# Feed-forward turns by 32-wide block transposes on VectorE and SBUF-to-SBUF transfers issued by GpSimd

## What is computed

```
def squared_relu_mlp(h, w1, w2):
    return jnp.square(jax.nn.relu(h @ w1)) @ w2      # w1: 2048 x 8192, w2: 8192 x 2048

x = x + squared_relu_mlp(rms_norm(x, norm_ffn_g[l]), w_ff1[l], w_ff2[l])
```

## Time and profile before

| what | value |
|---|---|
| runs of the kernel before | 1646.04 us median of 3 (1643.89 to 1647.24) |
| the profiled execution | 1646.18 us |
| its span | 1644.4 us |
| TensorE, matmuls busy | 1627.2 us, 99% of the span |
| VectorE busy | 1088.3 us, 66% |
| ScalarE busy | 811.9 us, 49% |
| GpSimd busy | 98.0 us, 6% (its DMA issues are not counted) |
| DMA | 304.91 MB, 185 GB/s over the span, of it 299.41 MB on SyncE's queue and 3.46 MB on GpSimd's |
| feed-forward stage | from about 945 us to about 1630 us |

### The profile page before, as it was taken

One profiled execution on the slowest core, in us unless ns is written; L12 is line 12 of the kernel. 1 busy time (PEld: TensorE's weight loads), 2 busy tenths in 40 slices (PEclk: granted clock), 3 DMA queues, 4 the chain that ended last, 5 costly groups with the idle time before them and its releaser, 6 DMA issues.

```text
span 1644.4 us, 21894 instructions
## 1 busy us (share of the span) xinstructions
PE 1627.2 (99%) x7524; PEld 1358.0 (83%) x7524; DVE 1088.3 (66%) x1476; ACT 811.9 (49%) x1063; POOL 98.0 (6%) x187
## 2 busy tenths in 40 slices
PE   9999999999999999999998999999999999999998
PEld 7888888888888888888887888888888888888886
DVE  5688988888888898665555655555555455545554
ACT  6444456555555556743445644434443444334443
POOL 6500011211111000000000000000000000000000
PEclk9999999999999999999999999999999999999999
DMA  7666655555555666557563566566656665566554
GB/s 249 207 185 187 190 160 159 174 169 181 172 155 172 221 201 182 189 180 268 177 194 115 168 182 190 191 194 190 186 188 191 191 182 188 193 192 184 192 184 142
DMA packets 158953, 304.91 MB, mean 185 GB/s; under 512 B 11658, under 2 KB 15874, under 8 KB 158466
## 3 DMA queue, kind: packets, MB, share of 16 engines
q1 hardware_dynamic: 157504, 299.41, 59.2%
q0 software_dynamic: 1056, 3.46, 0.6%
q10 hardware_dynamic: 320, 1.06, 0.2%
HBM read 301.78 MB, written 2.10 MB: 185 GB/s over the span
## 4 chain that ended last, share of the span: by engine, by line
PE 97%; ACT 1%; DVE 1%; issue 0%; POOL 0%; POOLq 0%; ACTq 0%
PE ps L1267 30%; PE ps L1269 30%; PE ps L1268 30%; PE ps L1280 2%; PE ps L1451 1%; PE ps L1450 1%; ACT hconv L750 0%; PE ps L1467 0%; PE ps L1461 0%; PE ps L1304 0%; PE ps L1555 0%; PE ps L1584 0%; PE ps L1583 0%; PE ps L1582 0%; PE ps L1468 0%
## 5 line engine op out<-in xcount | busy, mean ns | idle before, releaser
L868 DVE TENSOR_TENSOR wlo<-raw,whi 128x1024 fp32r<-128x1024 f32 x560 | 685.7, 1228 | 410.1 <-ACT whi L535 404.7
L535 ACT ACTIVATE whi<-raw 128x1024 fp32r<-128x1024 f32 x560 | 591.1, 1060 | 569.7 <-PE ps L1269 561.8
L1267 PE MATMUL ps<-whi,a_hi 128*128 128x512 f32 x1244 | 490.7, 394 | 0.6 <-issue 0.6
L1269 PE MATMUL ps<-whi,a_lo 128*128 128x512 f32 x1244 | 484.7, 390 | 0.0
L1268 PE MATMUL ps<-wlo,a_hi 128*128 128x512 f32 x1244 | 484.3, 389 | 0.0
L1267 PE MATMUL ps<-whi,c_hi 128*128 128x512 f32 x752 | 293.8, 391 | 0.0
L1269 PE MATMUL ps<-whi,c_lo 128*128 128x512 f32 x752 | 292.7, 389 | 0.0
L1268 PE MATMUL ps<-wlo,c_hi 128*128 128x512 f32 x752 | 292.6, 389 | 0.0
L1269 PEld LDWEIGHTS ps<-whi,a_lo 128*128 128x128 f32 x1244 | 233.5, 188 | 49.1
L1267 PEld LDWEIGHTS ps<-whi,a_hi 128*128 128x128 f32 x1244 | 233.7, 188 | 47.8 <-DVE wlo L868 1.2
L1268 PEld LDWEIGHTS ps<-wlo,a_hi 128*128 128x128 f32 x1244 | 233.8, 188 | 46.7
(11 more groups left out here) (240 smaller groups left out, 1081.8 us busy)
## 6 DMA issues: line engine op xcount, KB each, us to landing
raw<-in_w_ff_dram SPq DMA_DIRECT2D x256, 512.0 KB, 4.1
raw<-in_w_in_dram SPq DMA_DIRECT2D x144, 512.0 KB, 3.7
raw<-in_w_mla_out_dram SPq DMA_DIRECT2D x32, 512.0 KB, 4.6
raw<-in_w_conv_out_dram SPq DMA_DIRECT2D x32, 512.0 KB, 4.1
raw<-in_w_out_dram SPq DMA_DIRECT2D x32, 512.0 KB, 4.6
raw<-in_w_ukv_dram SPq DMA_DIRECT2D x16, 512.0 KB, 3.6
raw<-in_w_xkv_dram SPq DMA_DIRECT2D x16, 512.0 KB, 4.2
raw<-in_w_uq_dram SPq DMA_DIRECT2D x16, 384.0 KB, 3.7
```

Source lines behind the costliest of these rows:

```text
L535: act.activation(whi[:, s, :], raw[:, s, :], ACT.Copy).then_inc(hi_ready, 1)
L868: dve.tensor_tensor(wlo[:, s, :], raw[:, s, :], whi[:, s, :].bitcast(F32), ALU.subtract).then_inc(lo_ready, 1)
L1267: pe.matmul(sum_, x_hi[:, k0 + k, tok], w_hi, start=(first and k == 0), stop=False)
L1269: mm = pe.matmul(sum_, x_lo[:, k0 + k, tok], w_hi, start=False, stop=(last and k == kts - 1))
```

## The change

For the 16 chunks of the feed-forward stage, `turn` on TensorE goes. VectorE transposes each of its tokens-by-features tiles in 32x32 blocks from `rows` into `blocks` (two instructions of 128x512), GpSimd issues sixteen transfers from `blocks` to `moved`, each from one group of 32 partitions to another (32 rows of 1 KB), so that the blocks come to lie where a whole transpose would have them, and ScalarE and VectorE make `c_hi` and `c_lo` out of `moved` (128x512 each, twice per chunk), behind k = 4 where it was k = 3. TensorE waits for both parts of a turned chunk at once. SyncE's loads of w_ff1 are written without `load_chunk`. The turns of the other stages stay.

```diff
+QUAD = 32
+QUADS = P // QUAD
...
+        blocks = at(o, "blocks", [P, QUADS, CPB, TT, QUAD])
+        moved = at(o + 4096, "moved", [P, QUADS, CPB, TT, QUAD])
...
+        def quads(dst, c, t):
+            return dst[:, 4 * c:4 * c + 4, P * t:P * (t + 1)].rearrange("p k (i e) -> p k i e", i=QUADS)
...
                 for c in range(CH):
-                    load_chunk(U_FF + UPC * c, r, w_ff1, g * D + NC * c)
+                    for k in range(UPC):
+                        load(U_FF + UPC * c + k, r, w_ff1[:, 2 * k:2 * k + 2, ds(g * D + NC * c, NC)])
...
+            for g in range(GROUPS):
+                for c in range(CH):
+                    pool.wait_ge(blocks_ready, g * CH + (c + 1))
+                    for i in range(QUADS):
+                        for j in range(QUADS):
+                            pool.dma_start(moved[QUAD * j:QUAD * (j + 1), i, :, :, :], blocks[QUAD * i:QUAD * (i + 1), j, :, :, :]).then_inc(blocks_moved, 16)
...
-                        if k == 3 and c:
-                            turn_out(g * CH + (T_FF + c - 1), c_hi, 4 * (c - 1))
+                        if k == 4 and c:
+                            moved_out(g, c - 1)
...
-                        if k == 3 and c == 0:
-                            turn_out(g * CH + (T_FF + CH - 1), c_hi, 4 * (CH - 1))
+                        if k == 4 and c == 0:
+                            moved_out(g, CH - 1)
...
+            def moved_out(g, c):
+                act.wait_ge(blocks_moved, g * (16 * QUADS * QUADS * CH) + 16 * QUADS * QUADS * (c + 1))
+                for t in range(TT):
+                    act.activation(quads(c_hi, c, t), moved[:, :, :, t, :].rearrange("p i k e -> p k i e"), ACT.Copy).then_inc(turn_hi, 1)
...
+            def moved_low(g, c):
+                for t in range(TT):
+                    dve.wait_ge(turn_hi, g * (2 * CH) + (2 * (T_FF + c) + t + 1))
+                    dve.tensor_tensor(quads(c_lo, c, t), moved[:, :, :, t, :].rearrange("p i k e -> p k i e"),
+                                      quads(c_hi, c, t).bitcast(F32), ALU.subtract).then_inc(turn_lo, 1)
...
-                        if k == 3 and c:
-                            turn_low(g * CH + (T_FF + c - 1), c_lo, c_hi, 4 * (c - 1))
+                        if k == 4 and c:
+                            moved_low(g, c - 1)
                     p = pair_of(N_FF + c)
                     dve.wait_ge(relu_ready, g * CH + (c + 1))
                     dve.tensor_tensor(rows[:, p, :, :], rows[:, p, :, :], rows[:, p, :, :], ALU.mult).then_inc(chunk_out, 1)
+                    dve.wait_ge(chunk_out, g * (2 * CH) + (N_FF + c + 1))
+                    dve.wait_ge(blocks_moved, g * (16 * QUADS * QUADS * CH) + 16 * QUADS * QUADS * c)
+                    for t in range(TT):
+                        turned_blocks = dve.transpose(blocks[:, :, :, t, :].rearrange("p j k e -> p k j e"),
+                                             rows[:, p, t, :].rearrange("p (k j e) -> p k j e", k=CPB, j=QUADS))
+                    turned_blocks.then_inc(blocks_ready, 1)
...
-                        if k == 3 and c == 0:
-                            turn_low(g * CH + (T_FF + CH - 1), c_lo, c_hi, 4 * (CH - 1))
+                        if k == 4 and c == 0:
+                            moved_low(g, CH - 1)
...
-                        if c == CH:
-                            pe.wait_ge(turn_lo, g * (2 * CH) + (2 * splits_before(T_FF) + k + 1))
+                        if c == CH and k % 2 == 0:
+                            pe.wait_ge(turn_lo, g * (2 * CH) + (2 * splits_before(T_FF) + k + 2))
...
-                        if k == 3 and 1 <= c <= CH:
-                            pe.wait_ge(chunk_out, g * (2 * CH) + n)
-                            turn(None, rows[:, pair_of(n - 1), :, :], 0,
-                                 (turn_lo, g * (2 * CH) + (2 * splits_before(T_FF + c - 2) + 1)))
```

More of the change, by code:

```diff
@@ L329, in build @@
         tail_rooted, tail_rs, tail_gained = (sem(n) for n in ("tail_rooted", "tail_rs", "tail_gained"))
+        blocks_ready, blocks_moved = sem("blocks_ready"), sem("blocks_moved")
         fin_act, fin_dve, stored = sem("fin_act"), sem("fin_dve"), sem("stored")
+        def quads(dst, c, t):
+            return dst[:, 4 * c:4 * c + 4, P * t:P * (t + 1)].rearrange("p k (i e) -> p k i e", i=QUADS)
         block = ctx.enter_context(nc.Block())
```

## The result

The changed kernel takes 1650.05 us in the median (1644.23 to 1652.22, 18 runs); the kernel before took 1644.89 us on the same chips (1643.25 to 1648.13, 18 runs). The ratio is 1.0027, with a 95% interval of 1.0019 to 1.0034: slower by 0.27%, where the forecast was faster by 0.8%. The time lies inside the range of 1631 to 1682, whose upper part was made for issues dearer than they turned out. The profiled execution took 1646.85 us, its span is 1645.0.

What follows compares the result with a forecast made beforehand. TensorE, busy 99% of the span, was taken to bound the kernel: 1646.2 - 14.6 (sixteen turns gone) + 2.0 (four stalls of 0.5 us) = 1633.6 us. The range was 1631 to 1682 us.

Steps and rivals of the forecast that it cites:

- What vanishes: Feed-forward turns on TensorE: 16 turns (128 transposes) at 0.91 us each go, 14.6 us.
- VectorE and the issues: New path behind a chunk border: two VectorE transposes take 1.3 us, then sixteen GpSimd issues take 0.50 us each.
- rival 3: Feed-forward weight loads: bursts delay them until TensorE waits; delays of 8 us per burst end at 1646 us; chance 0.04.
- Rivals 1 and 2: GpSimd issues: 1, held up by VectorE, 1697 us, 0.16; 2, 0.74 or 0.86 us each, 1650 or 1679, shared 0.20.
- The landing: Last of a chunk's sixteen transfers: lands 3.1 us after its issue, with 2.7 and 6.2 us as the ends.
- the forecast's own formula: TensorE's stalls in all: 4 x (0.5 + D) + 12 x (D - 3.4) us, no bracket below zero.
- D: How much later the last transfer lands than 1029.8 us, the forecast landing behind the border at 1014.96.
- 3.4 us of slack: Turns other than a group's last: the turned chunk is ready 3.4 us before TensorE's next chunk holds up, so no stall.
- The two rows of 2.7 and 3.9 us: Earlier trace: small GpSimd transfers landed in 2.7 to 3.9 us at 246 GB/s; basis for taking 3.1 us.
- The row of 6.2 us: Landing of 512 KB from memory, kept as the upper end; gives D = 3.1 and 1646 us.
- part of 0.20: Chance of rival 2 and landings up to 6 us together: 0.04 faster, 0.07 within, 0.09 slower.
- break-even at D = 3.15: Where the 14.6 us gain and TensorE's stalls cancel; equals an issue of 0.71 us instead of 0.50.

Runs made afterwards that it cites:

- The first two experiments: Changed kernel with each group's last chunk turned by TensorE: 1633.07 us; changed kernel with fifth-chunk units 6 and 7 reading the third chunk's features, wait gone: 1631.14 us.
- the last: Changed kernel with eight of each chunk's sixteen transfers issued by ScalarE and eight by GpSimd: 1630.03 us, ratio 0.991 to the kernel before.
- the kernel with half rows: Changed kernel with each of the sixteen transfers carrying rows of 512 bytes instead of 1 KB: 1639.95 us, one run.
- the one with the extra burst: Changed kernel with one more burst of the same sixteen transfers, issued when no load is left: 1647.45 us, one run.

## Why the prediction was wrong, step by step

**What vanishes: right.** 16 x 0.91 = 14.6 us left TensorE. The first two experiments and the last give it back in the time to within 1.2 us (10.9 forecast and 11.4 measured for twelve turns; 14.6 and 13.4; 14.6 and 14.5).

**VectorE and the issues: right.** Groups of the kernel after by shape, 945 to 1640 us (busy us, mean ns, idle before):

```profile
L541 POOL DMA_DIRECT2D moved<-blocks x256 | 125.1, 497 | 662.8 <-DVE blocks L1251 552.5 <-issue 110.2
...
L1251 DVE STREAM_TRANSPOSE blocks<-rows 128x512 f32<-128x512 f32 x32 | 20.9, 691 | 1.3
...
L857 ACT ACTIVATE c_hi<-moved 128x512 fp32r<-128x512 f32 x32 | 18.4, 623 | 76.4 <-DMA moved<-blocks 76.4
```

The pair of transposes takes 1.31 us (taken: 1.3), an issue 0.497 (0.50), the pair of copies 1.15 (1.15). The nearest row was the right one for each. One start was late: GpSimd began one of the sixteen bursts 3.4 us behind its transposes (rival 3).

**Rivals 1 and 2 fall.** An issue of any of the 256 takes 0.496 to 0.534 us, with VectorE's subtractions beside some and not beside others, and 32 rows of 1 KB don't cost what 256 pieces of the earlier trace rows do. By the Trainium skill ("SBUF — State Buffer", Who interferes with whom) writing descriptors is inferred to need the shared write port, which a subtraction of two SBUF inputs doesn't take; the trace agrees, with issues of 0.496 us beside subtractions of 1.23.

**The landing: the term that failed.** The forecast took 3.1 us for the last transfer; the longest of each group's fourth burst was 6.3, 6.1, 5.6 and 5.3. By the forecast's own formula the mean of 5.8 gives D = 2.7 and stalls of 4 x (0.5 + 2.7) = 12.8 us; 13.5 were measured. The formula was right, and so was the claim that twelve turns have 3.4 us of slack: their longest landings, up to 5.7 us, are D = 2.6, and the one turn that ran out of slack did so by a late start of its issues (rival 3). The load on the engines had been worked out well too, at 192 + 66 = 258 GB/s; this window of the kernel after, the first burst with a stall, says 251, at the share of the earlier trace rows:

```profile
1014.70:1022.60 7.90, 7.90 (x36) 6.56 (x35) 4.44 (x4) 3.18 (x3) 7.81 (x16) 1.00 0.80 251
```

What failed is the step from an equal load to an equal landing. The two rows of 2.7 and 3.9 us were transfers of 8 KB among ten issues at the kernel's start; the transfers here carry four times that, sixteen in a row, beside loads of 512 KB. The row of 6.2 us stood beside them, was kept as an end, and was the nearer one: with D = 3.1 it makes stalls of 14.4 us, 13.5 were measured. That its 1646 us are also near the profiled 1646.85 is partly chance, since some 3 us of clock came on top and the base of 1646.2 had a fall of the clock of its own. Halving the other traffic brings 3.2 us, halving the burst's own 5.1, and taking all away 1.7 (five transfers): the landing belongs to what the engines carry, mostly the loads. The Trainium skill ("DMA: Bandwidth & Descriptors", Anatomy of one DMA) has 2.0 us + bytes / 436e3, an estimate of 2.1 us for 32 KB. That is near the 1.7 us of the five transfers with nothing beside them and fails beside the loads by a factor of up to three; the measurement decides.

**The clock: a term that wasn't in the sum.** The forecast priced a stall at its length. Behind stalls of 3.68 and 3.96 us TensorE's clock was at 1.2 GHz for 3.4 us, which cost 1.47 and 1.6 us; behind 3.19 and 2.69 it wasn't in this profile. The profiled execution is then 1644.89 - 14.6 + 13.5 + 3.1 = 1646.9 us beside 1646.85. Worked out from its counterpart of before, 1646.18, it would be 1648.2; but that execution had 3.4 us at half clock itself, at 891.98. For the median run four lengths make 1644.89 - 14.6 + 13.5 + 4 x 1.47 = 1649.7 us and five 1651.1, beside 1650.05 and a mean clock that asks for five or six. The same sum is 1.4 us too high for the kernel with half rows and 1.5 for the one with the extra burst. It closes to about 1.5 us, and how the median divides between stalls and clock no profile shows. It took both terms to turn the sign: with the measured stalls alone the sum is 1643.8, still a shade faster.

**Rival 3 fell as a cost, but its sign showed once.** It had the bursts delay the loads until TensorE waits for weights, and the text named a wait for `wlo` at the first unit of a chunk as the mark of D above 3.4. One came, in the third group, and neither a late load nor a long landing made it. Border, transposes, issues, copies and wait in the kernel after:

```profile
1304.12 0.39 PE L1300 MATMUL ps<-whi,a_hi 128*128 128x512 f32 x1
...
1306.98 1.31 DVE L1251 STREAM_TRANSPOSE blocks<-rows 128x512 f32<-128x512 f32 x2
...
1311.68 7.81 POOL L541 DMA_DIRECT2D moved<-blocks  x16 [109.49 <-issue]
...
1323.11 1.16 ACT L857 ACTIVATE c_hi<-moved 128x512 fp32r<-128x512 f32 x2 [6.85 <-DMA moved<-blocks]
...
1326.53 0.50 PE L1300 MATMUL ps<-whi,a_hi 128*128 128x512 f32 x1 [0.48 <-DVE wlo L889]
```

GpSimd starts 3.4 us behind the end of the transposes (1308.29) and waits for nothing that the profile shows. The copy finds the blocks 19.0 us behind the border, not 14.84, so D = 4.15, and the formula's 4.15 - 3.4 = 0.75 us of stall are 0.64 by distances between starts (1325.66 to 1326.53). The late start isn't an accident of one run: the ninth burst starts 3.4 us late in all profiles in which GpSimd issues whole bursts, also in the one with twelve bursts, where the ninth is the third group's third and TensorE's one wait for `wlo` stands behind it too (1360.67). It is the 129th issue that is late. The kernel in which ScalarE takes half of them has only 128 on GpSimd, and none is late so. Why isn't known. The raw loads did suffer from the bursts, though they made no wait: the five issued between 1014 and 1029 landed at a median of 6.8 us, while the earlier trace rows had 6.0 as the longest. Loads and bursts delay each other, and the bursts had the smaller slack.

**The chances.** The text had named the landing's upper end and its price. A landing of 5.3 to 6.3 us was given part of 0.20, and 0.11 of that stood on the side of faster or no change; once the clock is added the same case is a loss. The break-even at D = 3.15 was therefore too high: with 1.47 us on each of four stalls it is 4 x (0.5 + D + 1.47) = 14.6, D = 1.7, a landing of 4.8 us; with it on two of the four, as with half rows, D = 2.4, a landing of 5.5 us. The range held by luck: it reached to 1682 for issues of 0.74 and 0.86 us, which didn't come.

**Open.** Why the fourth burst of a group lands later than the three before it (longest 5.3 to 6.3 against 4.1 to 5.7 us) isn't settled. The DMA share doesn't order them: the window of the third group's first burst had 0.96 and landings of at most 4.1. So less traffic shortens the landing, but the traffic in the window alone doesn't set it. It isn't the stall either, since in the kernel without the wait the fourth bursts had 5.9 to 6.9 us and the others at most 5.4. Open, too, are which stalls the clock falls behind, and what holds up GpSimd's 129th issue.

## What to carry to other kernels

Price a transfer that somebody waits for by the longest landing of the trace beside the same loads, not by that of a smaller one; then ask which of its consumers has slack for that, and change only those. Of sixteen equal turns twelve were worth their gain and four lost all of it and more. A stall of some microseconds on TensorE costs more than its length where the clock falls behind it: find one such place in the trace and price it before the break-even is worked out, and look at more than one profile, since the third stall had none of it in one and 6.8 us of it in another. Where the issuing engine takes half the path, dividing the issues between two engines can be worth more than a faster transfer.

## What the runs showed of the hardware

- A transfer of 32 KB from SBUF to SBUF, issued by GpSimd, landed in 1.6 to 1.8 us with nothing beside it (five transfers), at a median of 2.6 us where the engines moved 110 GB/s in all, and 4.3 us (longest 6.3) at 200 GB/s in all.
- Seven of twelve stalls of 1.5 to 4.0 us in three profiles were followed by 3.4 us at the 1.2 GHz level (one by 6.8), the shortest of them 2.16 us long, while one of 3.19 was not. Where it was read matmul by matmul it cost 1.47 and 1.6 us. Matmuls in the stall's place kept the 2.4 GHz level.
- Issues of 32 rows of 1 KB took 0.496 us on GpSimd, one after the other, and eight of them on ScalarE took 5.15 us, 0.64 each.
- Two VectorE transposes of 128x512 in 32x32 blocks of float32 took 691 ns each, as long as a subtraction of that size (688 is that of `c_lo`).
